# A decoder trunk whose recurrent heads give VectorE fewer steps, with the normaliser states as a 129th column of the state products

## The reference

```python
b = jnp.cumsum(lf, axis=-1)
d = jnp.where(causal, b[..., :, None] - b[..., None, :] + li[..., None, :], -jnp.inf)
inter = b + m[..., None]
m_loc = jnp.maximum(inter, jnp.max(d, axis=-1))
w_intra = jnp.exp(d - m_loc[..., None])
w_inter = jnp.exp(inter - m_loc)
sw = jnp.einsum('bhtd,bhsd->bhts', qc, kc) * w_intra
num = w_inter[..., None] * jnp.einsum('bhtd,bhde->bhte', qc, c) + jnp.einsum('bhts,bhse->bhte', sw, vc)
qn = w_inter * jnp.einsum('bhtd,bhd->bht', qc, n) + jnp.sum(sw, axis=-1)
den = jnp.maximum(jnp.abs(qn), jnp.exp(-m_loc))
hc = num / den[..., None]
c_new = a[..., None, None] * c + jnp.einsum('bhs,bhsd,bhse->bhde', w, kc, vc)
n_new = a[..., None] * n + jnp.einsum('bhs,bhsd->bhd', w, kc)
...
hn = hc * lax.rsqrt(jnp.mean(hc * hc, axis=-1, keepdims=True) + EPS)
hn = hn.reshape(bt, t, A_HV) * g_head.astype(F32)
out = (jax.nn.sigmoid(o.astype(F32)) * hn).astype(h.dtype) @ w_out
```

## Time and profile before

| what | us |
|---|---|
| three runs | 1270.9, 1271.4, 1271.05 |
| median | 1271.05 |
| the profiled execution's own time | 1270.95 |
| its span | 1269.2 |
| PE busy | 1242.3 |
| DVE busy | 737.7 |
| ACT busy | 582.5 |

### The profile page before, as it was taken

How to read it: one execution, slowest core, us unless ns; L and a number is a source line. 1 busy time by engine, 2 the same in 40 slices (tenths; PEclk the granted TensorE clock), 3 DMA queues, 4 the chain that set the end, 5 groups by cost and what they waited for, 6 DMA issues and landing times.

```text
span 1269.2 us, 22196 instructions
## 1 busy us (share of the span) xinstructions
PE 1242.3 (98%) x8929; PEld 1217.6 (96%) x8929; DVE 737.7 (58%) x1156; ACT 582.5 (46%) x918; POOL 96.2 (8%) x117
## 2 busy tenths in 40 slices
PE   6999999999999999999999999999999999999996
PEld 6999999999889999999999999999996899999996
DVE  7565655565787655554555565654556576565433
ACT  7454533443455554533334554533443465454332
POOL 3000001100323000000000000000020110000011
PEclk9999999999999999999999999999999999999998
DMA  8434244633434444334543744334567743433441
GB/s 303 166 132 165 101 137 153 206 125 124 136 123 148 160 158 139 138 114 159 179 166 133 241 147 151 136 114 144 184 232 287 282 162 133 165 133 123 137 137 41
DMA packets 35994, 200.50 MB, mean 158 GB/s; under 512 B 4362, under 2 KB 6538, under 8 KB 20450
## 3 DMA queue, kind: packets, MB, share of 16 engines
q1 hardware_dynamic: 33858, 192.34, 43.7%
q0 software_dynamic: 2080, 7.39, 1.8%
HBM read 193.14 MB, written 6.57 MB: 157 GB/s over the span
## 4 chain that ended last, share of the span: by engine, by line
PE 92%; DVE 3%; issue 1%; ACT 1%; DMA 1%; SPq 0%; POOL 0%; POOLq 0%; DVEq 0%; ACTq 0%
PE bank L429 30%; PE bank L431 30%; PE bank L430 30%; DMA raw<-vc_in 1%; DVE cn L1495 0%; PE bank L539 0%; ACT junk L1059 0%; DMA raw<-w_in 0%; PE bank L550 0%; DVE dmat L1450 0%; PE bank L489 0%; DVE x L1729 0%; PE bank L761 0%; ACT dmat L1052 0%; DVE w_lo L1244 0%
## 5 line engine op out<-in xcount | busy, mean ns | idle before, releaser
L429 PE MATMUL bank<-h_hi,w_hi 128*128 128x320 f32 x1920 | 597.5, 311 | 11.5 <-DVE h_lo L1256 10.5
L431 PE MATMUL bank<-h_hi,w_lo 128*128 128x320 f32 x1920 | 594.1, 309 | 0.0
L430 PE MATMUL bank<-h_lo,w_hi 128*128 128x320 f32 x1920 | 594.1, 309 | 0.0
L919 ACT ACTIVATE w_hi<-raw 128x1024 fp32r<-128x1024 f32 (+1 forms) x368 | 335.8, 959 | 458.4 <-PE bank L431 454.2
L1244 DVE TENSOR_TENSOR w_lo<-raw,w_hi 128x1024 fp32r<-128x1024 f32 (+1 forms) x368 | 392.9, 1109 | 117.9 <-ACT w_hi L919 117.8
L429 PEld LDWEIGHTS bank<-h_hi,w_hi 128*128 128x128 f32 x1920 | 361.2, 188 | 14.1 <-DVE w_lo L1244 10.4
L430 PEld LDWEIGHTS bank<-h_lo,w_hi 128*128 128x128 f32 x1920 | 361.3, 188 | 0.4
L431 PEld LDWEIGHTS bank<-h_hi,w_lo 128*128 128x128 f32 x1920 | 361.2, 188 | 0.0
L430 PE MATMUL bank<-f_lo,w_hi 128*128 128x320 f32 x704 | 216.5, 308 | 0.0
L429 PE MATMUL bank<-f_hi,w_hi 128*128 128x320 f32 x704 | 216.5, 307 | 0.0
L431 PE MATMUL bank<-f_hi,w_lo 128*128 128x320 f32 x704 | 216.5, 307 | 0.0
(11 more groups left out here) (208 smaller groups left out, 616.5 us busy)
## 6 DMA issues: line engine op xcount, KB each, us to landing
raw<-w_in SPq DMA_DIRECT2D x88, 1024.0 KB, 4.8
raw<-w_out SPq DMA_DIRECT2D x64, 704.0 KB, 4.1
raw<-w_a SPq DMA_DIRECT2D x12, 1024.0 KB, 4.8
raw<-w_kv SPq DMA_DIRECT2D x8, 1024.0 KB, 4.8
raw<-vc_in SPq DMA_DIRECT2D x16, 512.0 KB, 6.4
raw<-kc_in SPq DMA_DIRECT2D x12, 512.0 KB, 4.7
raw<-w_oa SPq DMA_DIRECT2D x4, 1024.0 KB, 5.2
raw<-w_q SPq DMA_DIRECT2D x4, 1024.0 KB, 4.8
```

The source lines that it names most:

```text
L429: pe.matmul(out, wh, mh, start=first, stop=False)
L430: pe.matmul(out, wh, ml, start=False, stop=False)
L431: return pe.matmul(out, wl, mh, start=False, stop=last)
L919: sc.activation(w_hi[:, n_at % 2, part * w:part * w + w], raw[:, raw_of(n_at) % RAW, part * w:part * w + w], ACT.Copy).then_inc(hi_done, 1)
```

## The change

**In the heads.** The running sign change and maximum of the denominator on DVE (L1474, L1475, L1481, L1483) go. ACT squares the denominator column instead, and one DVE step takes the larger of its square and the square of the least value, `least`, which is made once for all heads. The exponential of a head is taken in three parts: the 128 columns of `dmat` from 128 to 255 need no cap, so ACT reads them from bank 4 with a bias, and DVE's first L1450 has 128 columns in place of 256. `gate_half` goes: `gated` adds 1 in its place, and half of the head's gain is applied in `z_split`. The copy L1502 moves from DVE to ACT, and the keys L1776 from POOL to DVE (`spread_keys`).

**The order.** On ACT the exponentials of head h + 1 stand ahead of the squares of head h. On DVE the decay and the queries of head h + 1 stand ahead of the variance of head h. On PE `spread_maxima` goes one head further ahead, behind the gate chunk, with a selector of 128 rows in place of 40. In the last turn two `z_split` stand ahead of the squares and two behind, and the turn of the last head goes from chunk 2 to chunk 5 of the first OA unit.

**The normaliser.** Both state products take the ones column of `v_tok` as their 129th column, so `n_new` comes out with `c_new`. The products of `n` at the end of the loop (L712, L713, L722), the four DVE steps after them and their DMAs go.

The core of the diff:

```diff
-        sel = sb("sel", [40, H, 128], f32r)
+        sel = sb("sel", [128, H, 128], f32r)
...
             def decay(h):
                 sc.wait_ge(d_done, h + 1)
-                sc.activation(dmat[:, :], dmat[:, :], ACT.Exp).then_inc(w_done, 1)
+                sc.wait_ge(qm_done, 2 * h + 2)
+                sc.activation(dmat[:, 128:256], bank[4][:, 128:256], ACT.Exp, bias=cols[:, 0, h:h + 1]).then_inc(w_done, 1)
+                for part in (slice(0, 128), slice(256, 448)):
+                    sc.activation(dmat[:, part], dmat[:, part], ACT.Exp).then_inc(w_done, 1)
 
             def head_squares(h):
 
                 sc.wait_ge(head_o, h + 1)
-                sc.wait_ge(den_done, h + 1)
+                if h >= 1:
+                    sc.wait_ge(s_in, h)
+                sc.activation(den[:, :].unsqueeze(2),
+                              bank[6][:, 0:3 * (DV + 1)].rearrange("p (t d) -> p t d", t=3)[:, :, DV:DV + 1],
+                              ACT.Square).then_inc(ssq_h, 1)
...
             for h in range(H):
-                head_squares(h)
                 if h + 1 < H:
                     decay(h + 1)
-                    head_scale(h)
                 else:
                     sc.wait_ge(unit_done, U_OA)
                     z_split(0)
                     z_split(1)
-                    head_scale(h)
-                    for g in range(2, H):
+                head_squares(h)
+                if h % 2 == 0:
+                    prompt_state(h)
+                if h + 1 == H:
+                    z_split(2)
+                    z_split(3)
+                head_scale(h)
+                if h + 1 == H:
+                    for g in range(4, H):
                         z_split(g)
                 for k, part in HALVES.get(h, ()):
                     split_half(U_A + k, U_A + k, loads_after(U_A + k), part)
...
             def variances(h):
 
-                ve.wait_ge(den_done, h + 1)
-                chain.link(ve.tensor_tensor(den[:, :].unsqueeze(2), den[:, :].unsqueeze(2),
-                                            cols[:, :, 96 + h:97 + h], ALU.max))
-                chain.link(ve.scalar_tensor_tensor(out=den[:, :], in0=den[:, :], scalar=EPS, in1=den[:, :],
-                                                   op0=ALU.mult, op1=ALU.mult))
-                ve.wait_ge(ssq_h, 3 * h + 3)
+                ve.wait_ge(ssq_h, 4 * h + 4)
+                chain.link(ve.scalar_tensor_tensor(out=den[:, :].unsqueeze(2), in0=den[:, :].unsqueeze(2), scalar=EPS,
+                                                   in1=least[:, :, h:h + 1], op0=ALU.mult, op1=ALU.max))
...
             def gated(h):
                 ve.wait_ge(ot_tr, h + 1)
-                ve.wait_ge(og_done, h + 1)
-                ve.scalar_tensor_tensor(out=og[:, h, :], in0=bank[3][:, 0:T],
-                                        scalar=par[:, P_HEAD + h:P_HEAD + h + 1], in1=og[:, h, :],
-                                        op0=ALU.mult, op1=ALU.mult).then_inc(z_done, 1)
+                ve.wait_ge(tanh_done, h + 1)
+                ve.scalar_tensor_tensor(out=og[:, h, :], in0=og[:, h, :], scalar=1.0, in1=bank[3][:, 0:T],
+                                        op0=ALU.add, op1=ALU.mult).then_inc(z_done, 1)
...
             def gated_at_kt(kt):
 
-                if kt == 2:
+                if kt == 5:
                     head_turn(H - 1)
-                    pe.matmul(bank[6][0:8, :], con[0:64, C_BM:C_BM + 8], kw[0:64, 2, :],
-                              start=True, stop=True).then_inc(n_mm, 1)
                 pe.wait_ge(hl_done, 2 * KT + kt + 1)
```

More of the change, by code:

```diff
@@ L653, in head_outputs @@
                     for t in range(2):
[L654 to L656 removed]
+                        for a in range(4):
+                            pe.matmul(bank[2][32 * a:32 * a + 32, 0:DV + 1], kw[:, t, h * 64 + 32 * a:h * 64 + 32 * a + 32],
+                                      v_tok[:, t, h + a // 2, :], start=(t == 0), stop=(t == 1),
                                       skip_group_check=True)
@@ L707, in _ @@
                     o_chunk(h + 1)
-                else:
-                    pe.wait_ge(p_done, H)
-                    for t in range(2):
-                        pe.matmul(bank[4][0:1, :], ones[:, 0:1], kw[:, t, :], start=(t == 0), stop=(t == 1))
-                    pe.matmul(bank[5][0:8, 0:8], con[0:64, C_LAST:C_LAST + 8], cols[0:64, 2, 64:72],
-                              start=True, stop=True)
+                    if h + 2 < H:
+                        spread_maxima(h + 2)
                 if h + 1 < H:
@@ L1023, in _ @@
             sc.wait_ge(dm_done, 1)
-            sc.activation(rows[64:72, 0:T], fa[:, :], ACT.Exp).then_inc(rows_b, 1)
             sc.activation(neg[:, T:384], fa[:, TP:T], ACT.Exp).then_inc(rows_b, 1)
@@ L1440, in _ @@
             ve.wait_ge(cols_done, 2)
+            chain.link(ve.scalar_tensor_tensor(out=least[:, :, :], in0=cols[:, :, 96:96 + H], scalar=EPS,
+                                               in1=cols[:, :, 96:96 + H], op0=ALU.mult, op1=ALU.mult))
             weigh_keys(0)
@@ L1528, in _ @@
                     spread_queries(h + 1)
-                    weights(h + 1)
-                    states(h)
+                else:
+                    z_split(0)
+                    z_split(1)
+                ve.wait_ge(head_o, h + 1)
+                if h + 1 < H:
+                    spread_keys(h + 1)
+                if h % 2 == 0:
+                    weights(h + 1)
+                variances(h)
+                if h % 2 and h + 1 < H:
+                    weights(h + 1)
+                if h + 1 == H:
+                    z_split(2)
+                    z_split(3)
+                states(h)
+                if h + 1 < H:
                     for k, part in HALVES.get(h, ()):
@@ L1534, in _ @@
                     gated(h)
-                    gate_half(h + 1)
                 else:
-                    z_split(0)
-                    z_split(1)
-                    states(h)
-                    for g in range(2, H - 1):
+                    for g in range(4, H - 1):
                         z_split(g)
```

135 lines of the change are left out of this document (55 added, 80 removed).

## The result

| kernel | median us | lowest to highest | ratio to before, 95% interval |
|---|---|---|---|
| before, beside the changed kernel | 1271.07 | 1270.9 to 1272.04 | |
| changed | 1275.27 | 1273.83 to 1275.64 | 1.0027 [1.0019, 1.0036] |
| changed, its profiled execution | 1274.91 | span 1273.1 | |

The account below looks back on a forecast made before the run. PE, 98% busy, bounds the kernel now; after the change a DVE, ACT and POOL ring of 8.18 us a head against 7.39, with a later end, adds 3.9 to 1270.95: 1274.85, median 1275.0, range 1271.5 to 1278.5.

Parts of the forecast that it names:

- The bound: Whole kernel: PE busy 98% of the span, with a DVE and ACT ring that PE just covers, 7.39 us a head.
- The ring: Head loop, DVE, ACT and POOL from first decay to first decay: 8.18 us a head against 7.39; chance 0.76.
- three exponentials: ACT, one head's exponential in three parts: 0.67 us, bounds 0.48 and 1.08; no row showed it.
- square of the denominator: ACT, 3 columns, ahead of the squares: 0.10 us, between 0 and 0.18; no row showed it.
- squares: Three squares on ACT, from the first to DVE's variance: 1.00 us, read from the earlier trace.
- power: POOL, 0.88 us and 0.04, now in the ring: 0.92; it formerly ran beside decays and exponential at no cost.
- Start and end: Decay 2 at 324.82, five rings, first OA matmul at 375.17, second OA unit about 385.3: +3.9 us.
- What I had said would show it: PE waits over 1 us before the turn, decays about 8.2 apart, DVE idle before w_lo, 2 us wait at second OA.
- The ring does not hold PE: Rival, head loop: PE's own list sets the time, 1267 to 1270 us; chance 0.09.
- Cheap and dear steps: Rivals, exponentials and small square at their bounds: cheap 7.89 a head, 1273.2 (0.13 with a milder end); dear 8.67, 1278.
- The clock: Rival: PE gaps of about 1.2 us a head cost it the full 2.4 GHz, above 1290 us; chance 0.02.
- The 129th column: State products, one more column: nothing to price; products of n leave PE where it waits, so bring nothing.

Follow-up runs that it names:

- The powers: Power of each head made twice on GpSimd: changed kernel 1281.53 us (1.0078), kernel before 1273.33 us (1.0017).
- the run with 40 rows: Kernel with ACT's half of w_hi ahead of the scaling, its spread selector cut from 128 rows to 40 again: 1270.86 us.
- two edits of order: Changed kernel with squares and variance ahead of the next head's exponentials and weights: 1268.85 us; or with ACT's half of w_hi ahead of the scaling: 1268.04 us.
- the changed kernel with two powers: Changed kernel with each head's power made twice on GpSimd, only the second announced: 1281.53 us, ratio 1.0078.
- the turn at chunk 4: Changed kernel with the turn of head 7 at chunk 4 instead of 5, nothing else: one execution, 1275.22 us.
- the two other orders: Kernel before with the column, 1273.11 us; w_hi ahead of scaling, head 7's turn at chunk 4, last z_split between halves: 1265.96 with column, 1269.04 without.
- the same steps in another order: Changed kernel with w_hi ahead of the scaling, head 7's turn at chunk 4, last z_split between the second OA unit's halves: 1265.96 us, 0.9957.
- the kernel with the column alone: Kernel before with only the normaliser as 129th column, products of n, their DVE steps and DMAs gone: 1273.11 us, 1.0015.

## Why the prediction was right

**The bound.** It was read rightly: PE's list sets the time before (no wait of PE in the loop), with a ring close behind. The powers put a number on close: 0.88 more in the ring cost 0.23 a head.

**The ring, item by item**, measured in the turn shown above:

| step | forecast | measured |
|---|---|---|
| decays, queries, handoff | 1.20 | 1.19 (1.33 in the other kind of head) |
| three exponentials | 0.67 | 0.72 |
| square of the denominator | 0.10 | 0.05 |
| squares | 1.00 | 0.91 |
| two small steps | 0.44 | 0.45 |
| power | 0.92 | 0.91 |
| scaling | 0.75 | 0.77 |
| w_hi | 1.10 | 1.09 |
| w_lo | 1.14 | 1.14 |
| gate, gated | 0.86 | 0.80 |
| **sum** | **8.18** | **8.03; 8.09 over five heads** |

Of the two terms that no row gave, the exponentials came out 0.05 above my value and the small square 0.05 below, so that their sum was right; the rule of the Trainium skill (ScalarE: Activation LUTs, "What ACT_TABLE_LOAD costs") had 0.75, near the 0.72 of this trace, and 0.10 for the small square, twice its 0.05. By either the sum was good to 0.2. The same three squares took 0.91 to DVE's next step, where they had taken 1.00 in the earlier trace rows: 0.08 of it lies between the end of ACT's last square and DVE's step (342.20 to 342.31 before, 343.79 to 343.82 here), and no row tells why.

**Start and end.** Decay 2 at 324.74 (forecast 324.82), the last gate chunk at 372.56 (373.04), the first OA matmul at 374.73 (375.17), chunk 4 at 379.07 (379.30), the second OA unit at 385.11 (385.3). My ring, 0.09 too long five times, gives the 0.44 to 0.48 up to the first OA matmul; the power of 1.22 in the last turn, where I had 0.88, took more than half of it back. That the end came out within 0.2 us is in part this luck of two errors with opposite signs.

**What I had said would show it.** ACT's scaling releases PE's waits, as I said, but they aren't all over 1 us: the two in the trace at 338.09 and 346.12 are 0.26 and 0.56, and the five come to 4.1. PE's own list is 6.67 us in one kind of heads and 7.25 in the other, so one ring of 8.09 leaves unequal gaps. I had put that list at 7.4, from the busy time of the earlier trace rows; it is 6.96 on average, and the new shape of the spread accounts for 0.34 of the 0.44 between, by the run with 40 rows. The gaps of 1.2 us a head in my rival on the clock don't follow from 8.18 and 7.4, which leave 0.8; 8.09 less 6.96 is 1.13, so that number was right by luck. The DVE idle ahead of `w_lo` (1.28, and 1.77 in the other heads; forecast 1 or more) and the wait for `w_lo` (1.61; forecast about 2) are there.

**The rivals.** *The ring does not hold PE*, 1267 to 1270: it is what two edits of order made (1268.85 and 1268.04), so its price was right and only its condition was not met. (The bound that it gave, a ring under 7.2 us, is 6.96 by the measured list.) *Cheap and dear steps*: the new steps came in between. *The clock*: in the profile of the changed kernel it is 1.00 in the loop, so it has no part in the result. But I gave the rival the wrong shape. I had only thought of a clock that is lost for good, above 1290; what the runs show is a spell of 3 to 7 us at 1.2 GHz after one wait, at a cost of nothing where PE had waits to spare (the changed kernel with two powers) and of some 1.5 us where 24 matmuls stood in it (the turn at chunk 4). The Trainium skill (TensorE: Matmul & The Clock Gate, Part 1) has such a fall and return as its rule; here it came behind waits of 1.68 to 2.27 us in four profiles, and waits of 1.68 to 2.29 us in others left the clock alone. *The 129th column*, "nothing I can price", was right for this order (1275.42 without it), by the reason given, but in the two other orders it is worth -1.6 and +3.1 us.

## What to carry to other kernels

Lighter steps on an engine that wasn't the bound gave nothing by themselves here: ask which operation now stands between two engines' lists, and put the work that needs none of it (here half a weight split) into the wait. Where a change takes work from the bound but makes it wait, sum both: the saved work comes back only once the wait is gone, which was worth 9.3 us here (1275.27 to 1265.96) with the same steps in another order. And price a part in the order in which it is to run, since one and the same column cost 1.6 us, nothing, or gained 3.1.

## What the runs showed of the hardware

- One matmul of 40 rows among matmuls of 128 rows costs some 0.3 us more than the same with 128 rows: 0.34 us a head, 2.8 us in all (1270.86 against 1268.04).
- After single waits of PE (1.91, 1.68, 2.27 and 1.72 us) the granted clock was 0.50 for 3 to 7 us in four profiles (matmuls 0.27 apart in place of 0.15). It stayed at 1.00 after 1.69 in the changed kernel, after 1.68 at 362.85 in the kernel with the column alone, and after 2.29 at 375.96 in the changed kernel with two powers. So the length of one wait doesn't tell whether the clock falls. With 2.08 us of useless products in such a wait, nine of eleven runs had a mean clock of 0.996 or more, against two of eleven without, and the time was no longer (1272.52 against 1273.11).
- A power of 128x3 on POOL lasts 0.88 us, and 1.22 or 1.23 in the last turn of the changed kernel and of the versions made from it, where a DVE step with two SBUF operands (an `h_lo`) starts 0.07 to 0.08 us ahead of it and runs beside it. In the kernel before, the `h_lo` (another instruction, two SBUF operands too) starts 0.04 behind it (372.10 and 372.06), and it lasts 0.88. Whether the start or the instruction makes the difference isn't shown.
- A load of 258 KB (the old state of head 6) lands in 3.2 to 3.9 us where the 1 MB load of weights next to it is issued 1.2 us or more behind it, in 5.6 to 5.8 us where one is issued within 0.3 us of it, and in 6.4 to 7.6 us where besides the store ahead of it in its queue has 258.0 KB in place of 256.0. The cause of the last step is open.
